# A two-layer decoder trunk: the gated-delta prelude, the expert choice and the zero rows reordered, and cross-attention's queries as three split products

## What is computed

```python
for l in range(DEPTH):                                   # 2
    h = rms_norm(x, norm_mix[l])
    # MoBA attention, S5 state space, gated DeltaNet from h @ w_in[l]
    q_g, k_g, v_g = jnp.split(silu(causal_conv(...)), 3, axis=-1)
    o_g = gated_delta_rule(l2_norm(q_g), l2_norm(k_g), v_g, log_decay, beta)
    x = x + merged @ w_out[l]
    x = x + cross_attention(rms_norm(x, norm_xa[l]), rms_norm(mem, norm_mem[l]),
                            xa_wq[l], xa_wk[l], xa_wv[l], xa_wo[l])
    h = rms_norm(x, norm_ffn[l])
    if l % 2 == 0:
        x = x + swiglu(h, ffn_w_gate[l // 2], ffn_w_up[l // 2], ffn_w_down[l // 2])
    else:
        logits = h @ w_router; top_val, top_idx = lax.top_k(logits, 2)
        top_w = jax.nn.softmax(top_val)                  # 8 experts, each d_ff = 2816
        x = x + sum_e(comb[..., e:e+1] * swiglu(h, w_gate[e], w_up[e], w_down[e]))
return rms_norm(x, norm_final)

def cross_attention(h, mem_n, wq, wk, wv, wo):
    q = (h @ wq).reshape(b_, s_, 4, 128)                 # wq: 1024 x 512
```

## Time and profile before

| | us |
|---|---|
| median of 3 runs | 1840.88 (1840.19 to 1843.71) |
| the profiled execution, as timed | 1838.29 |
| its span in the trace | 1836.5 |
| PE busy | 1748.5 (95%) |
| DVE busy | 1389.5 (76%) |
| ACT busy | 1047.1 (57%) |
| POOL busy | 163.4 (9%) |
| mean granted TensorE clock | 0.99 |

### The profile page before, as it was taken

How to read it: one execution, slowest core, us unless ns; L and a number is a source line. 1 busy time by engine, 2 the same in 40 slices (tenths; PEclk the granted TensorE clock), 3 DMA queues, 4 the chain that set the end, 5 groups by cost and what they waited for, 6 DMA issues and landing times.

```text
span 1836.5 us, 23533 instructions
## 1 busy us (share of the span) xinstructions
PE 1748.5 (95%) x9447; PEld 1406.7 (77%) x9447; DVE 1389.5 (76%) x1737; ACT 1047.1 (57%) x1202; POOL 163.4 (9%) x219
## 2 busy tenths in 40 slices
PE   7999998998999999998899799999999999999997
PEld 5687766686888788786667677888878787878785
DVE  5678678644555477876965488989898989989896
ACT  4234655454444423445644477777777767777775
POOL 6330002010000224000110010000000000000010
PEclk9999999999999999999999899999999999999999
DMA  8334522077462533442305589999999999999993
GB/s 254 138 136 140 183 92 93 8 275 249 146 205 91 156 136 138 151 171 95 136 2 194 195 324 375 393 371 374 380 372 390 357 389 357 390 356 391 346 397 124
DMA packets 216491, 434.90 MB, mean 237 GB/s; under 512 B 19193, under 2 KB 58241, under 8 KB 216385
## 3 DMA queue, kind: packets, MB, share of 16 engines
q1 hardware_dynamic: 208960, 415.78, 62.8%
q0 software_dynamic: 4560, 15.44, 2.1%
q10 hardware_dynamic: 2864, 2.23, 0.4%
HBM read 422.93 MB, written 10.49 MB: 236 GB/s over the span
## 4 chain that ended last, share of the span: by engine, by line
PE 79%; DVE 12%; ACT 5%; issue 3%; DMA 2%; POOL 0%; ACTq 0%; SPq 0%; DVEq 0%
PE bank L2991 14%; PE bank L2993 14%; PE bank L2992 14%; PE bank L2554 4%; PE bank L2574 3%; DVE split_e L1583 3%; PE bank L2578 3%; PE bank L2575 3%; PE bank L2496 2%; PE bank L2500 2%; PE bank L2497 2%; PE bank L2480 2%; PE bank L2473 2%; PE bank L2930 2%; PE bank L2746 1%
## 5 line engine op out<-in xcount | busy, mean ns | idle before, releaser
L1583 DVE TENSOR_TENSOR split_e<-ring,split_e 128x2048 fp32r<-128x2048 f32 x264 | 600.6, 2289 | 49.4 <-ACT split_e L1025 49.3
L1025 ACT ACTIVATE split_e<-ring 128x2048 fp32r<-128x2048 f32 x264 | 503.8, 1919 | 160.7 <-PE bank L2993 155.6
L2991 PE MATMUL bank<-split_e,fx_e 128*128 128x512 f32 x704 | 278.7, 396 | 2.0 <-DVE fx_e L2326 2.0
L2993 PE MATMUL bank<-split_e,fx_e 128*128 128x512 f32 x704 | 274.7, 390 | 0.0
L2992 PE MATMUL bank<-split_e,fx_e 128*128 128x512 f32 x704 | 274.2, 390 | 0.0
L2991 PEld LDWEIGHTS bank<-split_e,fx_e 128*128 128x128 f32 x704 | 132.2, 188 | 28.2 <-DVE fx_e L2326 2.2
L2993 PEld LDWEIGHTS bank<-split_e,fx_e 128*128 128x128 f32 x704 | 132.1, 188 | 28.2
L2992 PEld LDWEIGHTS bank<-split_e,fx_e 128*128 128x128 f32 x704 | 132.3, 188 | 26.2
L2991 PE MATMUL bank<-split_e,f_actT_e 128*128 128x512 f32 x352 | 138.7, 394 | 9.3 <-DVE f_actT_e L2334 9.3
L2993 PE MATMUL bank<-split_e,f_actT_e 128*128 128x512 f32 x352 | 137.1, 390 | 0.0
L2992 PE MATMUL bank<-split_e,f_actT_e 128*128 128x512 f32 x352 | 137.0, 389 | 0.0
(11 more groups left out here) (607 smaller groups left out, 3335.5 us busy)
## 6 DMA issues: line engine op xcount, KB each, us to landing
ring<-in_moe_w_gate SPq DMA_DIRECT2D x40, 2048.0 KB, 11.6
ring<-in_moe_w_up SPq DMA_DIRECT2D x40, 2048.0 KB, 11.5
ring<-in_moe_w_down SPq DMA_DIRECT2D x40, 2048.0 KB, 11.6
ring<-in_w_in SPq DMA_DIRECT2D x28, 2048.0 KB, 8.0
ring<-in_ffn_w_gate SPq DMA_DIRECT2D x11, 1024.0 KB, 5.6
ring<-in_ffn_w_up SPq DMA_DIRECT2D x11, 1024.0 KB, 8.1
ring<-in_ffn_w_down SPq DMA_DIRECT2D x11, 1024.0 KB, 8.8
ring<-in_ssm_w_glu SPq DMA_DIRECT2D x8, 1024.0 KB, 6.6
```

The costliest lines, as they stand in the source:

```text
L1025: nc.scalar.activation(split_e[j % NBUF][:, HI, :], ring[:, s * PIECE + i * HGRP:s * PIECE + (i + 1) * HGRP], ACT.Copy).then_inc(split_hi, 1)
L1583: V.tensor_tensor(split_e[j % NBUF][:, LO, :], ring[:, s * PIECE + i * HGRP:s * PIECE + (i + 1) * HGRP], split_e[j % NBUF][:, HI, :].bitca ...
L2991: mm(bank, a[HI], w[HI], start=first, stop=False)
L2993: return mm(bank, a[LO], w[HI], start=False, stop=last_one)
```

## The change

Four things are done together. (1) Queries: `U_WQ` becomes a split unit, ACT writes the normed x as fp32r (`xn_hi`) and DVE the rest (`xn_lo`), and `x_query` makes 24 products of 256 columns a head in place of 8 plain matmuls. (2) Zero rows: SP writes them from a strip of 256 zeros right behind the load of `U_OUT` of layer 0, and POOL's fill and DMAs go; with that, `step(0)` issues the down part of chunk 0 ahead of its wait for the queries. (3) Prelude: the last two taps of v, its tanh and its product move from ahead of the levels into levels 2 and 3, the keys' row factors come before the queries' on ACT and DVE, half of the second `memory_keys` comes after the key products, and the work beside the levels is gathered behind levels 2 and 4. (4) Choice: the best two are taken from the unscaled logits, `rstd` enters through the gather matrix (`taken`) and the weights; x times gain (`xg`) is written between the third and the fourth addition of w_o's output, `h_tok` later; the softmax weights (`token_weights`) come after the gather matrix.

The diff, cut (12 leading blanks are taken off each line):

```diff
+        WQ_HI = [[wq_u[:, :], wq_y[:, :], half_r(5), (wo_gate, wq_v)[a][:, :]] for a in range(2)]
+        xn_hi = over("xn_hi", [P, KD, SEQ], phase_at)
+        xn_lo = over("xn_lo", [P, KD, SEQ], phase_at + 4 * 9216)
...
+def zero_rows():
+    sp.wait_ge(xz_init, NT)
+    repeat = D // ZERO
+    for e in range(1, NE):
+        sp.dma_start(h_rows_d[e * SEQ:e * SEQ + P, :].rearrange("p (a n) -> p a n", n=ZERO),
+                     zero.unsqueeze(1).to_broadcast([P, repeat, ZERO])).then_inc(rows_set, 16)
+    sp.dma_start(y_rows_d[(NE - 1) * P:(NE - 1) * P + 1, :].rearrange("p (a n) -> p a n", n=ZERO),
+                 zero[0:1].unsqueeze(1).to_broadcast([1, repeat, ZERO])).then_inc(rows_set, 16)
...
+        if l == 0 and j == U_OUT:
+            zero_rows()
...
-        if i and c == 1:
+        if i and c < 2:
             down_(c, s)
-        if not i or c != 1:
+        if not i or c >= 2:
             down_(c, s)
+    sp.wait_ge(rows_set, 16 * (6 + NE))
...
-    if l == 0:
-        pool.wait_ge(wo_ps, 4)
-        link(nc.gpsimd.memset(h_e, 0.0))
-        for e in range(1, NE):
-            pool.dma_start(h_rows_d[e * SEQ:e * SEQ + P, :], h_e).then_inc(rows_in, 16)
-        pool.dma_start(y_rows_d[(NE - 1) * P:(NE - 1) * P + 1, :], h_e[0:1, :]).then_inc(rows_in, 16)
-        pool.wait_ge(rows_in, 16 * NE)
...
+    act.wait_ge(up_ps, 8 * l + 4)
+    first_taps(range(8, 12))
     conv_tanh(0)
     conv_tanh(1)
-    act.wait_ge(up_ps, 8 * l + 4)
     for i in range(4):
...
-    first_taps(range(8, 12))
-    keys_copy(0)
...
-    for i in (2, 3, 0, 1):
-        r_ = rq[i]
-        nc.scalar.activation(r_, r_, ACT.Exp, scale=-0.5).then_inc(cv_rs, 1)
+    def norm_rows(i):
+        nc.scalar.activation(rq[i], rq[i], ACT.Exp, scale=-0.5).then_inc(cv_rs, 1)
+    norm_rows(2)
+    norm_rows(3)
     act.wait_ge(dec_in, 3 * l + 1)
     nc.scalar.activation(dec[:, :], dec[:, :], ACT.Exp, scale=-1.0).then_inc(dec_ready, 1)
-    conv_tanh(2)
+    keys_copy(0)
+    norm_rows(0)
+    norm_rows(1)
     act.wait_ge(dec_in, 3 * l + 2)
     nc.scalar.activation(A21[GL:P], A21[GL:P], ACT.Exp, scale=-1.0).then_inc(dec_ready, 1)
-    keys_copy(1)
...
-        if k in (0, 2):
-            values_turned(k // 2)
-        if k == 1:
+        if k == 2:
             act.wait_ge(dec_in, 3 * (l + 1))
-            nc.scalar.activation(decT[:, 0:3], D4[:, 0:3], ACT.Exp).then_inc(dec_ready, 1)
+            nc.scalar.activation(decT[:, 0:3:2], D4[:, 0:3:2], ACT.Exp).then_inc(dec_ready, 1)
+        if k == 3:
+            conv_tanh(2)
+            keys_copy(1)
+        if k == 5:
+            values_turned(0)
+            values_turned(1)
...
+    def evac_queries(b):
+        act.wait_ge(norm_ps, 4 * n + b + 1)
+        for i, done in enumerate((x_hi, hT_ready)):
+            k = 2 * b + i
+            nc.scalar.activation(xn_hi[:, k, :], B[4 + b][:, i * SEQ:(i + 1) * SEQ], ACT.Copy,
+                                 scale=gain_xa[:, l * KD + k:l * KD + k + 1]).then_inc(done, 1)
+    unit_split_hi(l, U_WQ, range(4))
+    evac_queries(0)
+    evac_queries(1)
     unit_split_hi(l, U_WO, range(4))
-    evac_norm(n, xnT, gain_xa, l * KD, hT_ready, range(2, 4))
+    evac_queries(2)
+    evac_queries(3)
...
-    for w in range(1, 4):
-        taps(w, range(8, 12))
+    taps(1, range(8, 12))
...
+    row_scaled(0)
+    row_scaled(1)
...
-    silu(2)
+    row_scaled(2)
+    row_scaled(3)
...
+        if k == 1:
...
+        if k == 2:
+            taps(2, range(8, 12))
+            taps(3, range(8, 12))
+        if k == 3:
+            qk_decayed(1)
+            qk_decayed(2)
+            silu(2)
+        if k == 4:
             dve.wait_ge(gate_tanh, 2 * l + 2)
...
-    beside_level(5)
+    qk_decayed(0)
+    unit_split_lo(l, U_UPG, [0])
...
-    unit_split_lo(l, U_UPG, [2])
+    unit_split_lo(l, U_UPG, [1])
...
-    unit_split_lo(l, U_WO, range(4))
+        if i == 1:
+            unit_split_lo(l, U_WQ, range(4))
+        if i == 2:
+            query_rest(0)
+            query_rest(1)
+            unit_split_lo(l, U_WO, range(2))
+    query_rest(2)
+    query_rest(3)
+    unit_split_lo(l, U_WO, range(2, 4))
...
+            dve.wait_ge(gain_in, 32)
+            dve.wait_ge(xo_used, 4 * l + i + 1)
+            dve.wait_ge(xo_ps, 4 * (l + 1))
+            V.tensor_tensor(xg[:, t, :], x[:, t, :], gain_bc, ALU.mult).then_inc(h_gain, 1)
...
-        piece_lo("u", 0, 0, 0)
...
-        dve.wait_ge(gain_in, 32)
+        link(V.tensor_tensor(r_w[:, :, 0:1], r_max[:, :, 1:2], r_max[:, :, 0:1], ALU.subtract))
+        dve.wait_ge(norm_ss, 3 + 3 * l + 1)
+        dve.wait_ge(comb_ready, 1)
         for t in range(NT):
-            V.scalar_tensor_tensor(h_tok[:, t, :], x[:, t, :], rstd[:, t:t + 1], gain_bc, ALU.mult,
-                                   ALU.mult).then_inc(h_gain, 1)
+            V.tensor_scalar(taken[:, t, :], chosen[:, t, cols], rstd[:, t:t + 1], None, ALU.mult)
+        V.tensor_tensor(r_w[:, :, 0:1], r_w[:, :, 0:1], rstd.unsqueeze(2), ALU.mult).then_inc(rl_d, 1)
         dve.wait_ge(rl_ps, l // 2 + 2)
-        V.tensor_copy(place[:, :, cols], B[1][:, 0:NT * NE].rearrange("p (t e) -> p t e", t=NT))
-        link(V.tensor_reduce(e_most, B[1][:, NT * NE:NT * NE + NE], AX.X, ALU.max))
-        V.tensor_scalar(over_i[:, :], e_most, float(P), None, ALU.is_gt).then_inc(place_ready, 1)
+        V.tensor_copy(place[:, :, cols], B[1][:, 0:NT * NE].rearrange("p (t e) -> p t e", t=NT)).then_inc(place_ready, 1)
         dve.wait_ge(place_ready, 1)
...
+        def token_weights():
+            dve.wait_ge(rl_ps, l // 2 + 3)
+            link(V.tensor_reduce(e_most, B[3][:, 0:NE], AX.X, ALU.max))
+            V.tensor_scalar(over_i[:, :], e_most, float(P), None, ALU.is_gt).then_inc(place_ready, 1)
+            dve.wait_ge(rl_e, l // 2 + 1)
...
+            if p == 0:
+                piece_lo("u", 0, 0, 0)
+                token_weights()
             gathered_lo(n0)
...
-        if k == 0:
+        if k == 2:
+            memory_keys(1, 3, (1,), range(KD // 2, KD))
+            pe.wait_ge(kq_ready, 4 * (l + 1))
+            query_keys(1)
+            pe.wait_ge(a_ready, 2 * (l + 1))
+            query_keys(2)
+            pe.wait_ge(qk_ready, 4 * l + 1)
+            arrived(l, U_WV)
+            memory_values(0, [0, 1])
+        if k == 4:
+            pe.wait_ge(xk_sb, 8 * l + 2)
+            query_keys(0)
             pe.wait_ge(cv_ready, 3 * (l + 1))
-            turn_values(0)
-        if k == 1:
-            cross_keys()
-            pe.wait_ge(a_ready, 2 * (l + 1))
-            turn_values(1)
-        if k == 2:
-            pe.wait_ge(kq_ready, 4 * (l + 1))
-            pe.wait_ge(vt_evac, NT * l + 1)
-            query_keys(0)
-        if k == 3:
-            pe.wait_ge(qk_ready, 4 * l + 1)
-            query_keys(1)
-        if k == 4:
-            pe.wait_ge(vt_evac, NT * (l + 1))
-            query_keys(2)
+            for t in range(NT):
+                pe.wait_ge(qk_ready, 4 * l + 2 + t)
+                turn_values(t)
+            memory_values(0, [2, 3])
+    memory_keys(1, 3, (1,), range(KD // 2))
+    pe.wait_ge(xk_sb, 8 * l + 1)
+    cross_keys()
...
+        m0 = FIRST_SPLIT[U_WQ]
+        bank = B[XQ_BANK[h]][:, 0:SEQ]
+        def weights(v, k):
+            at = (k % 2) * 512 + h * XD
+            return (unit_lo(U_WQ, k // 2) if v == LO else unit_hi(l, m0 + k // 2))[:, at:at + XD]
         for k in range(KD):
             if h == 0 and k % 2 == 0:
+                pe.wait_ge(split_lo, unit_splits(l) + m0 + k // 2 + 1)
                 pe.wait_ge(hT_ready, 4 * (2 + 3 * l) + k // 2 + 1)
-            last = mm(B[XQ_BANK[h]][:, 0:SEQ], w[:, k, h * XD:(h + 1) * XD], xnT[:, k, :],
-                      start=k == 0, stop=k == KD - 1)
+            mm(bank, weights(HI, k), xn_hi[:, k, :], start=k == 0, stop=False)
+            mm(bank, weights(LO, k), xn_hi[:, k, :], start=False, stop=False)
+        for k in range(KD):
+            if h == 0 and k % 2 == 0:
+                pe.wait_ge(x_lo, xs_base(l) + X_XN + k // 2 + 1)
+            last = mm(bank, weights(HI, k), xn_lo[:, k, :], start=False, stop=k == KD - 1)
         last.then_inc(xk_ps, 1)
...
-        mm(B[1][:, 0:NE], before[:, :], chosen[:, 0, cols], start=True, stop=True)
-        mm(B[1][:, NE:2 * NE], ones[:, :], chosen[:, 0, cols], start=True, stop=False)
-        mm(B[1][:, NE:2 * NE], before[:, :], chosen[:, 1, cols], start=False, stop=True)
-        mm(B[1][:, 2 * NE:3 * NE], ones[:, :], chosen[:, 0, cols], start=True, stop=False)
-        mm(B[1][:, 2 * NE:3 * NE], ones[:, :], chosen[:, 1, cols], start=False, stop=True).then_inc(rl_ps, 1)
+        mm(B[1][:, 0:NT * NE], before[:, :], chosen[:, :, cols], start=True, stop=False)
+        mm(B[1][:, NE:2 * NE], ones[:, :], chosen[:, 0, cols], start=False, stop=True).then_inc(rl_ps, 1)
+        mm(B[3][:, 0:NE], ones[:, :], chosen[:, 0, cols], start=True, stop=False)
```

(1 more changed line is left out.)

## The result

The changed kernel took 1826.86 us (median of 4 runs, 1825.71 to 1828.05) where the kernel before took 1841.18 us (4 runs): a ratio of 0.9921, interval 0.9906 to 0.9937. The forecast was 1827.3 us. Its profiled execution was timed at 1828.05 us, with a span of 1826.2 us in the trace; the trace of before has 1836.5. So the two traces differ by 10.3 us, the medians by 14.3: the trace of before was of one of its faster executions (1838.29 us), that of the changed kernel of its slowest.

The account below looks back on a forecast made before the run. PE was taken to set the pace in the expert stage, with DMA waiting. Terms 5.4 + 3.2 + 1.0 + 4.0 = 13.6 us off the 1836.5 span gave 1822.9, plus 1.8 and 2.6: 1827.3 us, range 1819 to 1836.

Parts of the forecast that it names:

- What bounds the kernel: Expert stage: PE sets the pace, busy 689 of 700 us, DMA waits for places; two earlier stretches are loose.
- What is saved ahead of the stage is kept: Expert stage: since PE sets the pace there, time saved before it stays saved in full.
- Down part: Layer 0, w_o to dense layer: issuing chunk 0's down part earlier removes 3.7 us idle and 1.7 of low clock, -5.4.
- Zero rows: Moving their writes from POOL to SP's queue costs 0; bound +2 if the load of `U_OUT` came late.
- Queries: Cross-attention: 96 fp32r products at 0.122 us replace 13.8 us of plain matmuls; 1.6 of 2.1 us arrives a layer.
- rival (a): Queries: fp32r weight load bounds each product at 0.2285 us, +16.2 in place of -3.2, 1846.7 us; chance 0.12.
- Prelude: DeltaNet's prelude: level 0 starts 2.5 us earlier, but PE is full behind it; -0.5 a layer, bounds -2.5 and +1.5.
- Choice: Layer 1, choice of experts: experts start at 1053.9 instead of 1057.9 us, -4.0, bounds -4.6 and -2.5; gather stays 5.8.
- Sum: Whole kernel: the four gains make 13.6 us off the span of 1836.5, giving 1822.9 and a median of 1827.3.

Follow-up runs that it names:

- the first dummies: Changed kernel plus dummy matmuls on PE in layer 1's choice, 7 ahead of the last transposes and 9 behind the logits: 1826.45 us, ratio 0.9934.
- all together: Changed kernel plus norm factors' products first, dummy matmuls around and among the logits, 8 behind the gather, and token weights behind DVE's gathered rest: 1827.6 us, ratio 0.9932.
- the same dummies: Changed kernel plus dummy matmuls in the choice's two idle times and 7 more among the logits' short products: 1826.95 us, ratio 0.9926.

## Why the prediction was right, step by step

- **What bounds the kernel.** Held: the gains ahead of the dense layer reached layer 1 in full (191.95 against 191.96 us). "What is saved ahead of the stage is kept" was too strong for the experts: four traces whose experts start before 1047 us (the two of the changed kernel, the first dummies, all together) took 779.3 to 780.1 us for them, three others 778.0 to 778.5 (a fall of the clock worth 1.7 us taken off one of them), with late weights at the last expert as the difference; those that start later took 778.3 to 778.8. So 1 to 2 us may be given back there, and it is part chance.
- **Down part, -5.4.** Place, cause and size in the trace were right (5.47). As a mean it was too large: with the late issue the changed kernel lost 2.6 us in the stretch, and the part alone measured 3.1 (1.5 to 5.0). The weak step is that the sum took the 3.67 us of idle and the fall behind it in one execution for the rule, and put later falls of the clock at nothing; which of the two made the difference isn't shown.
- **Zero rows, 0.** Right, shown by the run that put them back.
- **Queries, -1.6 a layer.** 1.4 in both, shown by two traces of the changed kernel and by the undoing. The price of a product, between bounds that lay a factor of two apart, was 0.119 us: the type's 512-column row less its columns was the right neighbour, and rival (a), in which the weight load bounds it at 0.2285, is refuted. The Trainium skill's formula for an isolated matmul at the full clock ("TensorE: Matmul & The Clock Gate", section "Back-to-back issue gap") makes it 109 ns, an estimate; the trace has 119, so the two differ and the measurement decides. What the working had too large is the share that arrives: it let 1.6 of 2.1 us through, the traces 1.4 of 2.4. DVE's margin ahead of the third w_out addition was 0.43 us of idle time, as worked out (0.5).
- **Prelude, -0.5 a layer.** 0.9 and 0.7 between the two traces, 0.2 to 1.0 in layer 0 over all of them. The reading that PE is full behind the levels was right: its idle times from the key products' wait to the transposes sum to 2.8 us before and 2.2 after, as worked out. What the sum didn't have is the clock: in layer 1 the order before can lose 1.5 us more.
- **Choice, -4.0.** 4.0 between the two traces, with DVE's and the gather's times met within 0.3 us; between like parts of other traces 2 to 3.6. I wrote that the gather stays at the half clock, and it did.
- **Sum.** The terms made 13.6, the edited stretches 13.9, and the medians 14.3. That the last agrees is partly luck: the spans of the two traces differ by 10.3 us only, the other kernels' traces and runs point to less than the forecast for two terms (down part, choice), and to more for one (prelude in layer 1). Undoing them one by one gives ratios 0.9941 to 0.9946 against 0.9921 and 0.9930 for the whole, 2 to 5 us each with intervals of 3 us either way, so that the runs can't settle the sizes more finely than that.

**What stays open.** What makes the clock fall among the short products. It fell with PE gapless (twice), held in one execution with the same dummies, and when it held it fell later elsewhere. Neither idle time nor 8-column products alone explains that.

## What to carry to other kernels

Before you take a stall for a constant, ask which part of it is the granted clock of one execution: a stretch that holds no fall mostly repeats here within 0.1 us (the prelude of layer 0 within 0.8), one with a fall within 1 to 3 us, so a sum of terms should list the two kinds apart, and only the first kind can be forecast closely. Look along each issue queue for a transfer that stands behind a wait it has nothing to do with; moving two lines of it was the cheapest gain of this change. And read the margin of a streamed stage at its end too, where other transfers join: 2 MB more cost nothing in its middle, in the one trace that has them, while near its end weights came late in every trace.

## What the hardware showed that I had not expected

- An fp32r product of 256 columns starts 0.119 us behind the one before it, one of 512 columns 0.2285: two of the small ones cost about one large one, so the weight load that each of them has doesn't hold up the next product for longer than 0.119 us.
- The same instructions lose the full clock at different moments: layer 1's start took 19.7 to 21.3 us in twelve traces, the changed choice 31.3 in four and 32.9 in four others, never a value between.
- The clock fell to one half while PE was busy without a gap, with matmuls of 8 columns and with 128-column ones among them (7.99 of the 8 us before the fall in the kernel with dummies in the idle times), so a busy PE is no promise of the full clock.
- PE idle for 2.29 us ahead of level 0, the same wait in the same place, was followed by a fall in two of three traces in layer 1 and in none of three in layer 0; an idle time of 2.37 us in w_o was not, and one of 3.67 was.
